# One-hot tiles of the expert gates, built token by token with one scalar operand per token

## What is computed

```
q = (xt @ wq).reshape(T, PEER_HEADS, 2, PEER_HALF)
s = jnp.einsum('thpc,hpnc->thpn', q, subkeys)
s_top, i_top = lax.top_k(s, PEER_TOPK)                    # 16 of 128 keys on each half
cand = s_top[:, :, 0, :, None] + s_top[:, :, 1, None, :]
best, pos = lax.top_k(cand, PEER_TOPK)                    # 16 of 256 pairs
gates = jax.nn.softmax(best)                              # one gate per head and pick
act = gelu(einsum('cd,ced->ce', xb, u[eb])) * gb          # eb: expert numbers, gb: gates
y = einsum('ce,ced->cd', act, v[eb])
```

## Time and profile before

| | |
|---|---|
| median of three runs | 1826.32 us |
| the profiled execution | 1826.23 us, its span 1824.9 us |
| PE busy | 1739.2 us (95%) |
| DVE busy | 1091.1 us (60%) |
| ACT busy | 881.4 us (48%) |
| POOL busy | 502.4 us (28%) |
| expert_in loop | about 984 to 1462 us of the span |
| one-hots built | about 1105 to 1443 us |

### The profile page before, as it was taken

The page is one execution under the profiler, slowest core; times in us unless marked ns, Lnnn a source line. Parts: engine busy times, 40 slices in busy tenths (PEclk is TensorE's granted clock), DMA queues, the critical chain, the costliest instruction groups (busy, mean ns, idle before and its releaser), DMA issues.

```text
span 1824.9 us, 29105 instructions
## 1 busy us (share of the span) xinstructions
PE 1739.2 (95%) x11526; PEld 1582.3 (87%) x11526; DVE 1091.1 (60%) x1792; ACT 881.4 (48%) x1255; POOL 502.4 (28%) x274
## 2 busy tenths in 40 slices
PE   7978999999999999987999999999999999999997
PEld 5767999899999887865989999999999978888886
DVE  5665555376555463674144688797878555555555
ACT  5575544344444443754444444454444455554453
POOL 0544200030400042323532344343222232222221
PEclk9989999999999999988999999999999999999999
DMA  8333555554555543331344666555444577777775
GB/s 317 136 112 115 200 187 172 205 205 168 205 185 185 196 162 141 115 137 71 116 142 170 198 207 202 180 168 182 156 155 151 160 244 243 239 242 242 244 241 176
DMA packets 98071, 331.69 MB, mean 182 GB/s; under 512 B 10972, under 2 KB 44284, under 8 KB 79376
## 3 DMA queue, kind: packets, MB, share of 16 engines
q1 hardware_dynamic: 95904, 322.94, 52.4%
q0 software_dynamic: 2032, 6.89, 1.1%
HBM read 310.91 MB, written 18.87 MB: 181 GB/s over the span
## 4 chain that ended last, share of the span: by engine, by line
PE 81%; DVE 9%; ACT 5%; issue 2%; DMA 1%; POOL 1%; DVEq 0%; SPq 0%; ACTq 0%
PE banks L971 19%; PE banks L461 11%; PE banks L409 8%; PE banks L411 7%; PE banks L410 7%; PE banks L936 6%; PE banks L938 6%; PE banks L937 6%; PE banks L925 5%; PE banks L433 2%; ACT wH L996 2%; DVE wL L1521 1%; DVE qm L1859 1%; PE banks L678 1%; DMA raw<-in_qkv 1%
## 5 line engine op out<-in xcount | busy, mean ns | idle before, releaser
L2255 POOL TENSOR_TENSOR wL<-raw,wH 128x2048 fp32r<-128x2048 f32 (+1 forms) x59 | 221.2, 3760 | 649.1 <-ACT wH L996 649.0
L2053 DVE TENSOR_TENSOR uL<-raw,uH 128x1024 fp32r<-128x1024 f32 x192 | 243.9, 1270 | 224.5 <-ACT uH L1448 224.3
L409 PE MATMUL banks<-xH,wH 128*128 128x256 f32 x1216 | 344.7, 283 | 9.5 <-DVE xL L1548 9.5
L1448 ACT ACTIVATE uH<-raw 128x1024 fp32r<-128x1024 f32 x256 | 270.2, 1056 | 166.5 <-PE banks L971 166.5
L410 PE MATMUL banks<-xL,wH 128*128 128x256 f32 x1216 | 343.4, 282 | 0.0
L411 PE MATMUL banks<-xH,wL 128*128 128x256 f32 x1216 | 343.3, 282 | 0.0
L1521 DVE TENSOR_TENSOR wL<-raw,wH 128x2048 fp32r<-128x2048 f32 (+1 forms) x95 | 217.1, 2287 | 151.6 <-ACT wH L996 151.3
L996 ACT ACTIVATE wH<-raw 128x2048 fp32r<-128x2048 f32 (+1 forms) x154 | 269.7, 1762 | 78.5 <-PE banks L461 67.0
L936 PE MATMUL banks<-xH,uH 128*128 128x256 f32 x1024 | 296.0, 289 | 9.7 <-POOL uL L2289 7.5
L938 PE MATMUL banks<-xH,uL 128*128 128x256 f32 x1024 | 289.5, 283 | 0.0
L937 PE MATMUL banks<-xL,uH 128*128 128x256 f32 x1024 | 289.4, 283 | 0.0
(11 more groups left out here) (333 smaller groups left out, 2855.4 us busy)
## 6 DMA issues: line engine op xcount, KB each, us to landing
raw<-in_eu SPq DMA_DIRECT2D x128, 512.0 KB, 3.6
raw<-in_ev SPq DMA_DIRECT2D x128, 512.0 KB, 3.4
raw<-in_gu SPq DMA_DIRECT2D x44, 1024.0 KB, 4.8
raw<-in_dn SPq DMA_DIRECT2D x22, 1024.0 KB, 4.7
gelu_scratch<-st SPq DMA_DIRECT2D x128, 128.0 KB, 3.5
st<-gelu_scratch SPq DMA_DIRECT2D x128, 128.0 KB, 3.2
raw<-in_win SPq DMA_DIRECT2D x14, 1024.0 KB, 4.8
raw<-in_qkv SPq DMA_DIRECT2D x12, 1024.0 KB, 7.0
```

Source lines behind the costliest of these rows:

```text
L409: e.matmul(o, wh[:, w0:w0 + P], H[:, k, :], start=k == 0, stop=False)
L1448: e.activation(uH[n % US][:, :], raw[k // 2][:, (k % 2) * UW:(k % 2) * UW + UW], ACT.Copy).then_inc(s_uh, 1)
L2053: e.tensor_tensor(uL[n % US][:, :], raw[k // 2][:, (k % 2) * UW:(k % 2) * UW + UW], uH[n % US][:, :].bitcast(F32), ALU.subtract).then_inc( ...
L2255: e.tensor_tensor(wL[n % NS][:, c], raw[n % NR][:, c], wH[n % NS][:, c].bitcast(F32), ALU.subtract).then_inc(s_log, 1)
```

## The change

The one-hot tiles change their layout from [pick, value, token] to [pick, token, value], so that each token's 128 values lie together, and each is made by an instruction of its own: a comparison of iob (now 128 numbers) with one column of i2T, or with one column of i1T followed by a multiplication with one column of the gate part. The columns are operands of one element per partition. The tile oE and its two buffers go, and with them the wait between it and oA. i1T, i2T and the three gate parts are kept as f32; the multiplication's result is rounded to bf16 when it is written, so `picks_keep` needs two copies to bf16 instead of three. The matmuls of `gates` read both operands with a step of one. A batch of one-hots is now 16 instructions on 128 elements where it was 5 on 512.

```
-            for i in range(3):
-                e.tensor_copy(gp[i][:, tj], gT[:, tj]).then_inc(s_dv, 1)
+            for i in range(2):
+                e.tensor_copy(gp[:, :], gT[i][:, tj]).then_inc(s_dv, 1)
                 t = next(own)
                 e.wait_ge(s_dv, t)
-                if i < 2:
-                    e.tensor_tensor(gT[:, tj], gT[:, tj], gp[i][:, tj], ALU.subtract).then_inc(s_dv, 1)
+                e.tensor_tensor(gT[i + 1][:, tj], gT[i][:, tj], gp[:, :], ALU.subtract).then_inc(s_dv, 1)
...
-            e.tensor_tensor(oE[n][:, :, :], iob[:, :, :], wide(i1T), ALU.is_equal).then_inc(s_dv, 1)
-            t = next(own)
-            e.tensor_tensor(oB[n][:, :, :], iob[:, :, :], wide(i2T), ALU.is_equal)
-            e.wait_ge(s_dv, t)
-            for i in range(3):
-                r = e.tensor_tensor(oA[n][i][:, :, :], oE[n][:, :, :], wide(gp[i]), ALU.mult)
+            for m in range(GB):
+                c = slice(GB * bt + m, GB * bt + m + 1)
+                e.tensor_scalar(oB[n][:, m, :], iob[:, :], i2T[:, c], None, ALU.is_equal)
+                for i in range(3):
+                    r = e.tensor_scalar(oA[n][i][:, m, :], iob[:, :], i1T[:, c], gT[i][:, c], ALU.is_equal, ALU.mult)
             r.then_inc(s_hot, 1)
...
-                    r = e.matmul(ps[b][:, m * P:m * P + P], oB[n][:, :, m], oA[n][i][:, :, m], start=i == 0, stop=i == 2)
+                    r = e.matmul(ps[b][:, m * P:m * P + P], oB[n][:, m, :], oA[n][i][:, m, :], start=i == 0, stop=i == 2)
...
-        e.iota(flat2(iob[:, :, :]), [[1, P], [0, GB]], base=0, channel_multiplier=0, allow_small_or_imprecise_dtypes=True).then_inc(s_iob, 1)
+        e.iota(iob[:, :], [[1, P]], base=0, channel_multiplier=0, allow_small_or_imprecise_dtypes=True).then_inc(s_iob, 1)
```

More of the change, by code:

```diff
@@ L282, in build @@
     OG = o[0]
[L283 to L289, removed]
+    oB = [sb(f"oB{i}", [P, GB, P], BF16, off=o) for i in range(2)]
+    oA = [[sb(f"oA{n}{i}", [P, GB, P], BF16, off=o) for i in range(3)] for n in range(2)]
+    o = [OG + 10 * P * GB * 2]
+    i1T = sb("i1T", [P, S], off=o)
+    i2T = sb("i2T", [P, S], off=o)
+    gT = [sb(f"gT{i}", [P, S], off=o) for i in range(3)]
+    gp = sb("gp", [P, P], BF16, off=o)
     st = [sb(f"st{i}", [P, S], off=o) for i in range(4)]
-    iob = sb("iob", [P, P, GB], BF16, off=o)
+    iob = sb("iob", [P, P], BF16, off=o)
     GO = o[0]
@@ L2165, in picks_keep @@
             e.tensor_copy(i2T[:, tj], ps[j][:, P:2 * P])
-            e.tensor_copy(gT[:, tj], ps[j][:, 2 * P:3 * P]).then_inc(s_pkk, 1)
+            e.tensor_copy(gT[0][:, tj], ps[j][:, 2 * P:3 * P]).then_inc(s_pkk, 1)
             e.wait_ge(s_pkk, j + 1)
-            for i in range(3):
-                e.tensor_copy(gp[i][:, tj], gT[:, tj]).then_inc(s_dv, 1)
+            for i in range(2):
+                e.tensor_copy(gp[:, :], gT[i][:, tj]).then_inc(s_dv, 1)
                 t = next(own)
                 e.wait_ge(s_dv, t)
-                if i < 2:
-                    e.tensor_tensor(gT[:, tj], gT[:, tj], gp[i][:, tj], ALU.subtract).then_inc(s_dv, 1)
-                    t = next(own)
-                    e.wait_ge(s_dv, t)
+                e.tensor_tensor(gT[i + 1][:, tj], gT[i][:, tj], gp[:, :], ALU.subtract).then_inc(s_dv, 1)
+                t = next(own)
+                e.wait_ge(s_dv, t)
             sel[j] = t
         def hots(bt):
-            n, tt = bt % 2, slice(GB * bt, GB * bt + GB)
-            def wide(x):
-                return x[:, tt].unsqueeze(1).broadcast_to([P, P, GB])
+            n = bt % 2
             e.wait_ge(s_dv, sel[bt * GB // P])
```

## The result

The changed kernel takes 1879.46 us (median of four runs, 1874.73 to 1881.65) where the kernel before took 1826.69 us in the same session. The ratio is 1.0288, with a 95% interval of 1.0270 to 1.0306: 53 us slower. The forecast was 1850 us, 24 us slower. The profiled execution took 1879.11 us, its span 1877.7 us.

A forecast was written before the change was run, and what follows sets the result against it. PE was taken to bound the kernel, DVE with POOL passing its pace after the change: 7.6 us late, 12 us early and 4 us clock, 24 us on 1826.23, gave 1850 us; range 1824 to 1905 us.

The forecast's parts named there:

- What bounds it: In the expert_in loop PE sets the end, busy 179.0 of 179 us late; DVE and POOL come second.
- The price of an instruction: On DVE, each of 16 small one-hot instructions costs 0.168 us: 2.69 us per batch, 1.01 us more than before.
- 12 us for the early stretch: Early stretch: pairs with an eq pass or additions exceed PE's 7.12 us, plus stalls; 12 us taken between 6 and 17.
- 4 us for the clock: After each new stall PE's matmuls run slower, 1.4 us a time; with three stalls, +4 us.
- the dearer rival: One-hot instructions on DVE cost more, 3.47 us per batch if the second operand costs like the first: 1895 us; chance 33%.
- my 7.6: Late stretch: DVE plus POOL need 8.92 us a pair, 0.36 over PE's 8.56; 21 pairs give +7.6 us.
- The rival's own working with 3.2 us: Dearer case where bf16 saves nothing: 3.2 us per batch on DVE, 29 us late and some 20 more, 1880 us.
- The clash with POOL: The small DVE instructions and POOL's low parts exclude each other; several low parts of 5 us and more, PE idle for POOL.
- the stall of the earlier trace: Early stretch before the change: POOL's low part took 11.04 us behind dense DVE work, costing PE 5.41 + 1.4 us.
- PE's matmuls: Gate matmuls on PE: dense operands might save 0.08 us a batch, 5 us over 64; booked at nothing.
- The faster rival: DVE and POOL stay under PE at 0.10 to 0.13 us an instruction: 1821 us, or 1781 us by columns alone; chance 12%.
- 0.157: Late stretch: price in us per small DVE instruction at which the decision lies, a batch of 2.5 us, with PE as now.

The follow-up runs named there:

- e3: Kernel before, with only the moving operand (oA) of the gate matmuls read densely, weights keeping their step (wrong elements in G): 1783.47 us, ratio 0.9764.
- e12: Kernel before, with all low parts of the expert tiles made on DVE, none on POOL: 1813.43 us, ratio 0.9927.
- e5: Changed kernel, with oA made with one one-element operand, without the multiplication by the gate: 1821.32 us, ratio 0.9986.
- e4: Changed kernel, with the gate matmuls reading both tiles with the old step of four again (wrong elements): 1872.24 us, ratio 1.0252.
- e6: Changed kernel, with POOL subtracting only 32 of 1024 columns from the seventh expert tile on: 1790.50 us, ratio 0.9804.
- e1: Kernel before, with both operands of the gate matmuls read densely (wrong elements in G): 1786.64 us, ratio 0.9780.
- e8: Kernel before, with the moving operand of the gate matmuls read in runs of four elements (wrong elements): 1788.74 us, ratio 0.9798.
- e9: Kernel before, with the moving operand of the gate matmuls read in runs of two elements (wrong elements): 1826.18 us, ratio 1.0004.
- e10: Kernel before, with oE and oA laid out in runs of four per token, five large one-hot operations kept, all of the reference computed: 1790.68 us, ratio 0.9797.

## Why the prediction was wrong in size

**What bounds it: right.** PE set the end before; e3 gave back nearly all that was taken from PE, e12 what the one stall had cost.

**The price of an instruction: half right, and here the forecast failed.** I took 0.168 us for all 16, with the assumption that the second one-element operand is free, "because it needs the fewest assumptions beside rows 5". The price with one operand was 0.163 us, about as the sum had it; its parts, bf16's halving among them, were not measured apart. The second operand, with its multiplication, costs 0.060 us more, nearly the 0.065 us that I had worked out for the first. A batch takes 3.33 us, not 2.69, and 3.47 was written down as the rival's price "if the second operand cost as much as the first". e5 shows that this term is worth 46 us by the starts of the instructions, 50 between the profiled executions and 58 between the medians: about the whole slowdown. At 2.61 us a batch the changed kernel would have taken 1821.32 us, and at my 2.69 some 5 us more by an estimate (64 x 0.08). So at my own price 1850 us would have been too high by some 24 us: the sum's 12 us for the early stretch and 4 us for the clock had no counterpart there. The two errors lay on opposite sides. The chance for the dearer rival (33%) should have been the larger one: three quarters of the instructions had a form that no row showed, and the row nearest to a second operand was that of the first.

**The sum with the right price.** A late pair is 1.14 + 2 x 3.33 + 2.2 = 10.0 us, and 10.02 us was measured. That is 1.44 us over 8.56, 30 us for the 41 late batches in the place of my 7.6, and 29.8 us was measured: the late stretch comes out whole, without a term for the clock.

**The early stretch: an overlap that was not there.** I had 12 us, and 25.5 were measured. I let the pairs without a pass or an addition go free, since "most route steps don't exclude POOL": one low part, one batch and POOL's turn are 1.14 + 3.33 + 2.2 = 6.7 us even at the right price, under PE's 7.12, with the route steps beside POOL. But in the changed kernel POOL's turn fell on the one-hots and not on the route steps, and all of it stood in a row on DVE: low part 1.13, route steps 1.83, one-hots and turn 5.45, together 8.4 us from 1139.64 to 1148.05. Nearly every pair from the third batch on lost time, and not the six that I had counted. In e4, and in e5 at about my price, the overlap held and these pairs kept PE's pace (7.1 and 6.4 us); why POOL's turn moved in the changed kernel was not tested.

The rival's own working with 3.2 us gave 1880 us, and 1879 was measured. That is luck in part: its reason there (bf16 saves nothing) was the wrong one.

**The clash with POOL: right that it is there, wrong in its form.** e6 shows it at its full size, 89 us. I expected POOL to be kept out by dense DVE work, low parts of 5 us and more, and PE waiting for POOL. Instead POOL nearly always got in at once, and PE waited for oA (70.2 us) and hardly for POOL's low parts (3.4 us). The form makes no difference to the sum in the late stretch, as DVE and POOL share one budget either way. In the early stretch it does: the stall of the earlier trace rows, from which I extrapolated, did not come back in this form, and the ordinary pairs became dearer instead.

**PE's matmuls: booked at 0 (5 us at most), really 43 to 45 us, and hidden.** I took the 0.112 us of the earlier trace rows as a sign that 128 columns have this price by themselves. Those are f32 matmuls; the bf16 ones are at half of it when dense. The argument for leaving the term out (a faster PE only waits longer) was right for this kernel, and e4 shows it. At a lower price part of the gain would have come through: in e5 the early pairs ran at 6.4 us instead of 7.1. The faster rival's 1781 us was never near, though e3 measured such a time (1783.47) with the large one-hots. Dense matmuls bring PE's pair down to some 7.16 us, and for PE to set the end at that pace a small instruction may cost (7.16 - 1.14 - 2.2) / 2 / 16 = 0.12 us by an estimate, not 0.157. e5, at 0.163 us, took 1821.32.

**Clock.** The granted clock fell from 1.00 to 0.93 in the late stretch, with 36 waits for oA where I had booked three stalls; how many microseconds that is was not measured by itself. In the late stretch the sum comes out without it.

## What to carry to other kernels

Before a few large operations are broken into many small ones, price the exact form: each one-element operand counts, and the fixed part counts as often as there are instructions. Then ask which part of a change helps by itself: here the layout was worth 43 us and its making cost more, and a layout in short runs got most of the gain (35 us) without the price. Add the time in which one engine locks out the other to the budget of both, above all when the engine that had room becomes the bound; and count it as overlapped only where the trace shows on which instructions it falls.

## What the runs showed of the hardware

- The moving operand of a bf16 matmul of 128 columns read with a step of four elements makes it take 0.116 us instead of 0.056; the same step in the weights costs nothing (e1 to e3). Runs of four elements are enough, runs of two are not (e8, e9).
- A tensor_scalar on 128 bf16 elements takes 0.163 us with one one-element operand and 0.223 us with two (changed kernel, e5).
- A 2.38 us subtraction on POOL holds back a small tensor_scalar on DVE for 2.2 us, some 40 times in one kernel, and with it the end (e6). POOL gets in at once between small instructions, and in other places waits up to 13.94 us for two (e10). What decides between the two was not settled.
- A route step's MATCH_REPLACE8 on DVE keeps its 0.27 us while POOL subtracts (e4); the same turn of POOL costs 2.1 us where it falls on the one-hots and 0.8 us where only its end does.
